# Gated delta rule: inverses written to the other half of the rows, four corners of the array, and copies moved to ScalarE

## The reference, cut to what matters

```python
lower = jnp.where(strict, jnp.einsum('bhnid,bhnjd->bhnij', kb, k) * decay, 0.0)
tmat = lower + jnp.eye(c, dtype=jnp.float32)
sol = lax.linalg.triangular_solve(tmat, rhs, left_side=True, lower=True, unit_diagonal=True)
u, w = sol[..., :dv], sol[..., dv:]
```

## Time and profile before

| | us |
|---|---|
| median of 3 runs | 1902.21 (1901.73 to 1903.26) |
| the profiled execution | 1899.6 |
| its span, first to last instruction | 1897.8 |
| busy: PE, DVE, ACT, POOL | 1735.9, 824.1, 719.2, 601.9 |
| mean granted clock of PE | 0.966 |

### The profile page before, as it was taken

The page is one execution under the profiler, slowest core; times in us unless marked ns, Lnnn a source line. Parts: engine busy times, 40 slices in busy tenths (PEclk is TensorE's granted clock), DMA queues, the critical chain, the costliest instruction groups (busy, mean ns, idle before and its releaser), DMA issues.

```text
span 1897.8 us, 32340 instructions
## 1 busy us (share of the span) xinstructions
PE 1735.9 (91%) x13588; PEld 1399.4 (74%) x13588; DVE 824.1 (43%) x1481; ACT 719.2 (38%) x1115; POOL 601.9 (32%) x318
## 2 busy tenths in 40 slices
PE   6899999969989898898899977988899899999996
PEld 2788888847878676677877747986578588888885
DVE  0301366375330266556647478564514533333112
ACT  3425223244353533444535864014433432222222
POOL 0222322391323323731034305013234244444442
PEclk9899999999999999998999998999999899999998
DMA  8344311310222111313422200001121122232331
GB/s 331 118 164 137 119 47 37 112 32 23 66 90 69 65 57 57 112 34 111 134 78 89 83 18 2 4 2 45 45 89 34 56 91 99 92 97 95 101 104 67
DMA packets 42569, 152.17 MB, mean 80 GB/s; under 512 B 4416, under 2 KB 5568, under 8 KB 42176
## 3 DMA queue, kind: packets, MB, share of 16 engines
q1 hardware_dynamic: 38880, 140.72, 22.0%
q10 hardware_dynamic: 3552, 9.44, 1.4%
HBM read 145.95 MB, written 4.19 MB: 79 GB/s over the span
## 4 chain that ended last, share of the span: by engine, by line
PE 42%; DVE 7%; ACT 2%; issue 2%; DVEq 0%; ACTq 0%
PE wide_ps L1785 29%; PE wide_ps L1807 2%; PE pair_ps L2361 1%; PE wide_ps L2358 1%; PE wide_ps L2337 1%; PE wide_ps L2296 1%; DVE xn L1553 1%; PE duo_ps L2465 1%; PE wide_ps L2446 1%; DVE xn L1703 1%; PE wide_ps L1822 1%; PE pair_ps L1861 1%; DVE ring_r L1192 1%; PE pair_ps L2296 0%; DVE h L1707 0%
## 5 line engine op out<-in xcount | busy, mean ns | idle before, releaser
L535 POOL TENSOR_TENSOR ring_r<-ring,scratch_r 128x1024 fp32r<-128x1024 f32 x177 | 428.4, 2421 | 1001.7 <-ACT scratch_r L707 974.8
L1785 PE MATMUL wide_ps<-xn_r,scratch_r 128*128 128x512 f32 x1272 | 470.5, 370 | 0.0
L1785 PE MATMUL wide_ps<-work_r,scratch_r 128*128 128x512 f32 (+1 forms) x1109 | 427.7, 386 | 5.2 <-ACT proj L694 5.2
L1785 PE MATMUL wide_ps<-work_r,ring_r 128*128 128x512 f32 (+1 forms) x1109 | 412.6, 372 | 0.0
L707 ACT ACTIVATE scratch_r<-ring 128x1024 fp32r<-128x1024 f32 x193 | 204.5, 1061 | 531.3 <-PE wide_ps L1785 453.0
L1785 PEld LDWEIGHTS wide_ps<-xn_r,scratch_r 128*128 128x128 f32 x1272 | 240.5, 189 | 47.5 <-issue 5.4
L1785 PEld LDWEIGHTS wide_ps<-work_r,scratch_r 128*128 128x128 f32 x1109 | 208.9, 188 | 53.3 <-ACT proj L694 9.9
L1785 PE MATMUL wide_ps<-proj_r,scratch_r 128*128 128x512 f32 x704 | 238.1, 386 | 1.6 <-DVE proj_r L1184 1.6
L1785 PEld LDWEIGHTS wide_ps<-work_r,ring_r 128*128 128x128 f32 x1109 | 209.0, 188 | 38.8
L694 ACT ACTIVATE proj<-wide_ps 128x512 f32<-128x512 f32 (+2 forms) x116 | 74.0, 638 | 222.0 <-PE wide_ps L1785 205.6
L1785 PEld LDWEIGHTS wide_ps<-proj_r,scratch_r 128*128 128x128 f32 x704 | 132.9, 189 | 31.4 <-DVE proj_r L1184 2.3
(11 more groups left out here) (408 smaller groups left out, 2996.9 us busy)
## 6 DMA issues: line engine op xcount, KB each, us to landing
ring<-weights SPq DMA_DIRECT2D x256, 512.0 KB, 3.5
h<-tokens SPq DMA_DIRECT2D x4, 768.0 KB, 11.7
h<-tokens ACTq DMA_DIRECT2D x1, 3072.0 KB, 10.0
out<-h ACTq DMA_DIRECT2D x1, 2048.0 KB, 7.3
h<-out ACTq DMA_DIRECT2D x1, 2048.0 KB, 10.8
out<-h SPq DMA_DIRECT2D x8, 256.0 KB, 2.0
const_sb<-const SPq DMA_DIRECT2D x1, 1089.0 KB, 6.1
h<-mem ACTq DMA_DIRECT2D x1, 1024.0 KB, 13.2
```

The source lines that it names most:

```text
L535: pool.tensor_tensor(as_r(wt), wt, as_r(w_lead(m)).bitcast(F32), ALU.subtract).then_inc(w_split, 1)
L1785: last = pe.matmul(wide_ps[:, bank, a:b], wt[:, cols], as_r(x[:, a:b]), start=n == 0 and p == 0, stop=n == len(k_order) - 1 and p == 2)
```

## The change

- The half products (from level 1), the first kind of products and the products of level 0 now write to the other half of the partitions, the crossed corners; the second kind stays on the straight ones. `dn_inv` of a block therefore lies on the other half than its `dn_inv_t`. The corner products swap likewise.
- Level 0: the identity is a new constant `idents` on both halves, so `dn_inv_t` is one subtraction over 128 rows, and the step's signal `dn_y` comes behind it. PE turns `dn_inv_t` instead of `dn_half`, and ACT copies the result to `dn_inv` (new semaphore `dn_t0`).
- ACT takes over the copies of keys and values.
- The near quarters (`near_corners`) are scaled ahead of the wait for the corner products.

```diff
@@ -105,7 +105,7 @@
 CONST2_COLS, N_CONST2 = table([("tri0", P), ("tri1", P), ("inv0", (LEVELS - 1) * HD), ("inv1", (LEVELS - 1) * HD),
-                               ("window", 3 * P), ("rot_half", P), ("inv_freq", 1)])
+                               ("window", 3 * P), ("rot_half", P), ("inv_freq", 1), ("idents", HD)])
@@ -415,6 +415,10 @@
 
+        def inverse_done(engine, q):
+            engine.wait_ge(*((dn_t0, q) if q <= 4 else (dn_t, q - 4)))
@@ -464,6 +468,7 @@
         dn_y_ps, dn_y, dn_z_ps, dn_t = (sem(n) for n in ("dn_y_ps", "dn_y", "dn_z_ps", "dn_t"))
+        dn_t0 = sem("dn_t0")
@@ -1078,6 +1083,12 @@
                     act.activation(e, e, ACT.Exp, scale=-1.0).then_inc(dn_e_ready, 1)
+                act.wait_ge(dn_tok_ps, n + 1)
+                act.activation(k_tok_2(c), by_head(dn_bank(6)), ACT.Copy)
+                act.activation(v_tok_2(c), by_head(dn_bank(7)), ACT.Copy).then_inc(dn_tok, 1)
+            for q in range(4):
+                act.wait_ge(dn_z_ps, q + 1)
+                act.activation(dn_inv(q), dn_bank(4 + q % 2), ACT.Copy).then_inc(dn_t0, 1)
@@ -1588,11 +1599,8 @@
                     dve.tensor_tensor(dn_qk(u), kq, e, ALU.mult).then_inc(dn_x, 1)
-                dve.wait_ge(dn_tok_ps, n + 1)
-                dve.tensor_copy(k_tok_2(c), by_head(dn_bank(6)))
-                dve.tensor_copy(v_tok_2(c), by_head(dn_bank(7))).then_inc(dn_tok, 1)
-            ident_8 = [cst["ident"][rows, rows].unsqueeze(1).broadcast_to([HD, 8, HD]) for rows in HALF]
+            idents_8 = cst2["idents"].unsqueeze(1).broadcast_to([P, 8, HD])
@@ -1604,13 +1612,13 @@
                 if 2 <= q < 6:
-                    dve.wait_ge(dn_t, q - 1)
-                dve.tensor_tensor(to_8(dn_half(p)), to_8(dn_bank(p % 2)), mask, ALU.mult).then_inc(dn_y, 1)
+                    dve.wait_ge(dn_y, q - 1)
+                masked = dve.tensor_tensor(to_8(dn_half(p)), to_8(dn_bank(p % 2)), mask, ALU.mult)
                 if l == 0:
-                    dve.wait_ge(dn_y, q + 1)
+                    link(masked)
                     dve.wait_ge(dn_qg, DN_GROWN[NLAT - 1])
-                    for r, rows in enumerate(HALF):
-                        dve.tensor_tensor(to_8(dn_inv_t(p))[rows], ident_8[r], to_8(dn_half(p))[rows], ALU.subtract)
+                    masked = dve.tensor_tensor(to_8(dn_inv_t(p)), idents_8, to_8(dn_half(p)), ALU.subtract)
+                masked.then_inc(dn_y, 1)
@@ -1618,15 +1626,18 @@
                 dve.wait_ge(dn_z_ps, q + 1)
-                if l == 0:
-                    to_8 = lambda v: v.rearrange("p (n t) -> p n t", t=HD)
-                    for r, rows in enumerate(HALF):
-                        ins = dve.tensor_tensor(to_8(dn_inv(p))[rows], ident_8[r], to_8(dn_bank(4 + p % 2))[rows], ALU.subtract)
-                else:
-                    mine, other_side = (lambda v: halves(v, 1 << l)[:, :, side, :]), (lambda v: halves(v, 1 << l)[:, :, 1 - side, :])
-                    dve.tensor_tensor(mine(dn_inv_t(p)), mine(dn_inv_t(p)), mine(dn_bank(2 + p % 2)), ALU.subtract)
-                    ins = dve.tensor_tensor(other_side(dn_inv(p)), other_side(dn_inv(p)), other_side(dn_bank(4 + p % 2)), ALU.subtract)
-                ins.then_inc(dn_t, 1)
+                mine, other_side = (lambda v: halves(v, 1 << l)[:, :, side, :]), (lambda v: halves(v, 1 << l)[:, :, 1 - side, :])
+                dve.tensor_tensor(mine(dn_inv_t(p)), mine(dn_inv_t(p)), mine(dn_bank(2 + p % 2)), ALU.subtract)
+                dve.tensor_tensor(other_side(dn_inv(p)), other_side(dn_inv(p)), other_side(dn_bank(4 + p % 2)),
+                                  ALU.subtract).then_inc(dn_t, 1)
+            def near_corners(n):
+                for s in (2 * n, 2 * n + 1):
+                    for d in range(2):
+                        u, lo = dn_unit(d, s), HALF[0]
+                        factor = beta[:, chunk_at(d, s), 4 * d:4 * d + 4].unsqueeze(2).broadcast_to([P, 4, HD])
+                        dve.tensor_tensor(dn_lower(u)[lo, :, lo], by_head2(dn_inv_t(u // 2), s)[lo], factor[lo], ALU.mult)
@@ -1634,9 +1645,8 @@
                         u, c = dn_unit(d, s), chunk_at(d, s)
-                        lo, to = HALF[0], HALF[d]
+                        to = HALF[d]
                         factor = beta[:, c, 4 * d:4 * d + 4].unsqueeze(2).broadcast_to([P, 4, HD])
-                        dve.tensor_tensor(dn_lower(u)[lo, :, lo], by_head2(dn_inv_t(u // 2), s)[lo], factor[lo], ALU.mult)
@@ -1645,8 +1655,11 @@
                     half_masked(q)
-                if q:
+                if q > 4:
                     inverse_update(q - 1)
+            dve.wait_ge(dn_t, steps - 4)
+            for n in range(2):
+                near_corners(n)
@@ -2327,14 +2340,15 @@
                 else:
-                    pe.wait_ge(dn_t, q - 3)
+                    inverse_done(pe, q - 3)
...
                 for m in range(8):
-                    for rows in HALF:
+                    for r, rows in enumerate(HALF):
...
                         inv_t = dn_inv_t(p)[rows, HD * m:HD * m + HD] if l else cst["ident"][rows, rows]
-                        last = pe.matmul(dn_bank(p % 2)[rows, HD * m:HD * m + HD], x, inv_t, start=True, stop=True, skip_group_check=True)
+                        to = HALF[1 - r] if l else rows
+                        last = pe.matmul(dn_bank(p % 2)[to, HD * m:HD * m + HD], x, inv_t, start=True, stop=True, skip_group_check=True)
@@ -2346,16 +2360,16 @@
                 if q >= 2:
-                    pe.wait_ge(dn_t, q - 1)
+                    inverse_done(pe, q - 1)
...
                     if l == 0:
-                        for rows in HALF:
-                            last = pe.matmul(dn_bank(4 + p % 2)[rows, at], dn_half(p)[rows, at], cst["ident"][rows, rows], start=True,
+                        for r, rows in enumerate(HALF):
+                            last = pe.matmul(dn_bank(4 + p % 2)[HALF[1 - r], at], dn_inv_t(p)[rows, at], cst["ident"][rows, rows], start=True,
...
                         continue
-                    for rows in HALF:
-                        pe.matmul(halves(dn_bank(2 + p % 2)[rows, at], 1 << l)[:, :, side, :], dn_inv(p)[rows, at],
+                    for r, rows in enumerate(HALF):
+                        pe.matmul(halves(dn_bank(2 + p % 2)[HALF[1 - r], at], 1 << l)[:, :, side, :], dn_inv(p)[rows, at],
@@ -2370,20 +2384,20 @@
             for n in range(2):
-                pe.wait_ge(dn_t, steps - 2 + 2 * n)
+                inverse_done(pe, steps - 2 + 2 * n)
...
                         frm, to, p = HALF[1 - d], HALF[d], 2 * n + d
-                        last = pe.matmul(dn_bank(6 + n)[to, HD * m:HD * m + HD], dn_lower(2 * p + m // 4)[frm, m % 4, to],
+                        last = pe.matmul(dn_bank(6 + n)[frm, HD * m:HD * m + HD], dn_lower(2 * p + m // 4)[frm, m % 4, to],
...
                     for d in range(2):
-                        to, p = HALF[d], 2 * n + d
-                        last = pe.matmul(dn_bank(n)[to, HD * m:HD * m + HD], dn_inv(p)[to, HD * m:HD * m + HD],
-                                         dn_corner(n)[to, HD * m:HD * m + HD], start=True, stop=True, skip_group_check=True)
+                        frm, to, p = HALF[1 - d], HALF[d], 2 * n + d
+                        last = pe.matmul(dn_bank(n)[to, HD * m:HD * m + HD], dn_inv(p)[frm, HD * m:HD * m + HD],
+                                         dn_corner(n)[frm, HD * m:HD * m + HD], start=True, stop=True, skip_group_check=True)
@@ -2588,7 +2602,7 @@
                         + [np.where(t >= s, 0, NEG), np.zeros((P, P)), np.where(t <= s, 0, NEG), rotation(halves),
-                           np.tile(inv_freq, 4)[:, None]], 1)
+                           np.tile(inv_freq, 4)[:, None], np.tile(np.eye(HD), (2, 1))], 1)
...
 

```

## The result

| | before | after |
|---|---|---|
| median, 4 runs each in turn | 1901.97 us (1900.59 to 1903.26) | 1884.84 us (1881.73 to 1888.71) |
| the profiled execution | 1899.6 | 1881.73 |
| its span | 1897.8 | 1879.9 |

The ratio is 0.9911, with a 95% interval of 0.9891 to 0.9931: 17.1 us faster, where 29.8 were forecast. The time lies just above the range.

The account below looks back on a forecast made before the run. DVE was taken to bound decay and level 0, PE levels 1 to 5. Gains of 0.8 + 8.0 + 18.7 + 2.3 = 29.8 us gave a median of 1872 us, range 1862 to 1884, chance 0.84.

Parts of the forecast that it names:

- Levels 1 to 5: 20 steps of the inverses after level 0: four corners cut a step from 2.80 to 1.93 us, gaining 18.7 us.
- rival 1: In levels 1 to 5 row halves take turns on a bank or PE's instructions come too slowly; 1889 us, chance 0.09.
- Rivals 2 and 3: Crossed pairs sharing a bank go singly, 1930 us, chance 0.04; PE stays at 1.2 GHz in levels, 1906 us, 0.03.
- Level 0: First four steps of the inverses: one subtraction over 128 rows replaces two, 10.2 us instead of 18.2, gaining 8.0 us.
- Corners: After the levels: near quarters scaled while PE multiplies the corner products, gaining 2.3 us.
- Decay: Stage before the first mask: key and value copies move from DVE to ACT, gaining 0.8 us.

Follow-up runs that it names:

- a_straight: The changed kernel with every 64x64 call back on the straight corners, the rest of the change kept; 1883.86 us, ratio to before 0.9913.
- g1_full: Changed kernel on straight corners, half products from level 2 as 8 calls of 128 rows instead of 16 of 64, weights block diagonal; 1902.29 us.
- e_more: The changed kernel with each product of the second kind issued twice in levels 1 to 5, 256 instructions a step; 1902.32 us, ratio 1.0009.
- b_cross: The kernel before with the crossed corners alone, no other part of the change; 1898.75 us, ratio 0.9989.

## Why the prediction was wrong

- *Levels 1 to 5, the step that failed.* The prediction put "64 product records take 1.00 us instead of 1.87" and "a step becomes 1.93 us". The first half is right (0.97 us, and a step of 1.86 or 1.87 us at the full clock where no border falls into it). The second took for granted that a faster array is a shorter step. A step has 192 instructions, and they arrive in 2.7 us: a wait for instructions that the sum had put at nothing. So 4.5 us came instead of 18.7. Of these, 2.4 came in a_straight too (57.3 us for the levels), with none of them at the half clock, and the 2.1 that the crossing adds there did not show in the time of the kernel.
- *Where the profile could have told it.* The rate of L1905 in the earlier trace rows was read from rows of 48 records, and the prediction noted itself that those bursts are short, but gave this 0.09 together with the bank. The DMA view of the stage before, which I did not read, has the line that bears on it: 13 blocks of instructions in 50 us, one in 3.8 us, with 256 instructions used in 3.73. This proves no limit, since blocks come as they are used: g1_full, with 160 instructions in 3.91 us, has 9 in 50 us. But a step of 1.93 us asks for a block in 2.6 us, and the closest two transfers in the whole trace before start 3.4 us apart. So the rate that the forecast needed had never been seen for longer than a burst, and the sum 192 / 2.80 stood in rival 1.
- *Rival 1* was right in its second half, PE's instructions, and gave 1889. Measured is 1884.8, since decay and levels gave 0.8 and 2.5 more than it allowed. Its first half, the turns on a bank, is not what happened: with shared banks four corners ran 15.2 ns a record.
- *Rivals 2 and 3.* A crossed pair alone keeps its rate: whole groups of 32 crossed half products start within 0.90 to 0.96 us, 29 to 31 ns each, against 0.91 us in a_straight. The clock was 1.00 from 1206 to 1226; it was at half only from 1184.3 to 1187.6 in these levels.
- *Level 0*: 7.7 of 8.0. Right, by its own steps; the subtraction over 128 rows took 1.04 to 1.75 us, as those over 64.
- *Corners*: 2.4 of 2.3, in part by luck: that the far ones took 0.45 each and not 0.34 was offset by the near ones at 0.50 instead of 0.6.
- *Decay*: 1.6 of 0.8. ScalarE's copies follow each other every 0.48 us, not 0.60, so that six of them, 2.9 us, just fill its waits of 2.82 us. Its last exponential ends 19.0 us after its first operation of the stage (1143.40 us here), where the prediction had 20.0 and the kernel before 19.2. Two such copies, and the last exponential of the stage, before DVE's last unit:

```profile
1147.16 0.63 ACT L1087 ACTIVATE scratch<-duo_ps 128x512 f32<-128x512 f32 x1
1147.63 0.64 ACT L1088 ACTIVATE proj<-duo_ps 128x512 f32<-128x512 f32 x1
...
1161.55 0.86 ACT L1085 ACTIVATE xn<-xn 128x512 f32<-128x512 f32 x1
```

What stays open: what sets the 3.7 us between blocks. The transfer is not the whole of it: the window from 1204.8 to 1210.5 us holds one, with 1.6% of 16 engines' time, 0.016 x 16 x 5.7 = 1.5 us on the one engine that brings it. The trace of e_more, where PE stands at every border, splits the time further. By the starts of PE's records and of the transfers, as means over 19 borders: PE begins a block, 1.3 us later a transfer starts, it takes 1.2 us, and PE begins the next block 1.4 us (1.2 to 1.6) after it has landed, 3.9 us in all. So one block at a time is on its way, and over two thirds of the time are spent before and behind the transfer. That PE waits for just this transfer is read from the order and the steady 1.4 us. No run changed the blocks themselves.

## What to carry to other kernels

Count the instructions of an engine in the stretch, not only its busy time: where PE's calls are as small as 64x64 with 32 or 64 columns, the stretch can be no shorter than its instructions take to arrive, here 14.7 ns each, and a faster way to execute them only makes gaps. What helps is fewer instructions of the same width: a transpose in place of sixteen products gave, on four corners, what four corners alone could not. When two limits coincide before a change, as 96 records x 29.2 ns and 192 instructions x 14.6 ns did, lifting one shows the other, so look for the second before pricing the first.

## What the runs showed of the hardware

- PE's instructions come in blocks of 16 KB, 256 instructions, one per 3.7 to 3.9 us at the fastest; when they are used faster, PE stands for 0.7 to 1.7 us behind nearly every block (up to 2.0 in b_cross), and starts again 1.4 us after the transfer has landed (e_more). Bursts inside a block run at 9 to 10 ns an instruction (250 in 2.3 to 2.6 us).
- Four corners of 64x64 give a record every 15.2 ns even when both halves of the rows write to the same bank on different partitions.
- A 128x128 weight with 64 columns of data costs 116 ns a record, where one of two alternating corners of 64x64 gives a record in 58 ns and four corners together one in 15.2 ns.
- A transpose of 128x128 shows as one record of PE and one weight load where a product of 32-bit floats shows as two of each, so a group's sixteen blocks turn in 8 instructions instead of 64.
